# Prefix scan of a gated linear-attention trunk: rows reversed, modulation moved into the weights

## What is computed

```python
h = rmsnorm(x, norm1_g) * (1 + sc1) + sh1
k = h @ W_k ;  a = h @ W_a                        # 4 heads of 128; rank 16
la = log_sigmoid(a @ w_alpha + b_alpha) / 16      # one decay per key channel
S_t = exp(la_t)[:, None] * S_{t-1} + k_t^T v_t    # per head, 128 x 256
```

## Time and profile before

| | us |
|---|---|
| median of 3 executions | 1438.56 (1438.42 to 1439.32) |
| the profiled execution | 1442.98 |
| its span on the slowest core | 1441.4 |
| busy in it: PE, DVE, ACT, POOL | 1333.1, 688.4, 504.3, 109.8 |

### The profile page before, as it was taken

The page is one execution under the profiler, slowest core; times in us unless marked ns, Lnnn a source line. Parts: engine busy times, 40 slices in busy tenths (PEclk is TensorE's granted clock), DMA queues, the critical chain, the costliest instruction groups (busy, mean ns, idle before and its releaser), DMA issues.

```text
span 1441.4 us, 22660 instructions; the slowest of 8 cores (1428.5 to 1441.4 us)
## 1 busy us (share of the span) xinstructions
PE 1333.1 (92%) x7660; PEld 695.5 (48%) x7660; DVE 688.4 (48%) x1257; ACT 504.3 (35%) x1122; POOL 109.8 (8%) x208
## 2 busy tenths in 40 slices
PE   1577999998989899889999999999999999999997
PEld 1333445444545455544445555555555445555443
DVE  1467557543656577642233334962122552212486
ACT  1576456432445455431211112981111001111233
POOL 3000100000000000011110120010000002000000
PEclk9778999998999999999999999999999999999999
DMA  9736401206211111154342366532223006222222
GB/s 173 212 117 154 52 9 30 52 2 59 51 23 23 23 23 23 23 96 73 52 74 38 62 102 135 179 68 37 40 35 44 1 1 103 36 40 35 59 103 110
DMA packets 42797, 92.66 MB, mean 64 GB/s; under 512 B 5206, under 2 KB 8166, under 8 KB 42684
## 3 DMA queue, kind: packets, MB, share of 16 engines
q0 software_dynamic: 29264, 53.02, 24.9%
q1 hardware_dynamic: 13420, 38.20, 8.2%
HBM read 133.95 MB, written 10.25 MB: 100 GB/s over the span
## 4 chain that ended last, share of the span: by engine, by line
PE 74%; ACT 9%; DMA 5%; DVE 5%; issue 5%; POOL 0%; ACTq 0%; DVEq 0%; SPq 0%; POOLq 0%
PE psum L464 72%; ACT sb_arena L447 6%; DMA sb_wring<-wfm 2%; DVE sb_arena L450 2%; PE psum L467 2%; ACT sb_tmpB L447 2%; DMA sb_wring<-w_in 1%; ACT sb_rstd L447 1%; DMA sb_wring<-w_mod 1%; DVE sb_arena L454 1%; DVE sb_arena L458 1%; DMA sb_arena<-xm 1%; DVE sb_tmpB L458 0%; POOL sb_wring L437 0%; DVE sb_arena L455 0%
## 5 line engine op out<-in xcount | busy, mean ns | idle before, releaser
L464 PE MATMUL psum<-sb_arena,sb_wring 128*128 128x384 bf16 (+3 forms) x4448 | 837.5, 347 | 11.5 <-DVE sb_arena L461 10.1
L464 PEld LDWEIGHTS psum<-sb_arena,sb_wring 128*128 128x128 bf16 x4448 | 430.1, 98 | 385.3 <-issue 44.2
L464 PE MATMUL psum<-sb_wring,sb_arena 128*128 128x512 bf16 (+2 forms) x1596 | 350.4, 378 | 4.3 <-DMA sb_wring<-w_in 4.3
L447 ACT ACTIVATE sb_tmpB<-psum 128x384 f32<-128x384 f32 (+1 forms) x264 | 139.6, 532 | 606.3 <-PE psum L464 576.1
L450 DVE TENSOR_TENSOR sb_arena<-psum,sb_tmpB 128x384 bf16<-128x384 f32 (+5 forms) x254 | 148.6, 587 | 324.6 <-PE psum L464 306.1
L464 PEld LDWEIGHTS psum<-sb_wring,sb_arena 128*128 128x128 bf16 (+1 forms) x1596 | 155.8, 99 | 184.0 <-issue 7.4
L437 POOL DMA_DIRECT2D sb_wring<-wfm x140 | 75.3, 545 | 912.5 <-PE psum L464 769.0
L450 DVE TENSOR_TENSOR sb_tmpB<-psum,sb_tmpB 128x384 f32<-128x384 f32 (+2 forms) x80 | 47.8, 598 | 171.0 <-PE psum L464 170.5
L450 DVE TENSOR_TENSOR sb_arena<-psum,sb_arena 128x512 f32<-128x512 f32 (+2 forms) x106 | 72.6, 685 | 35.3 <-PE psum L464 35.1
L447 ACT ACTIVATE sb_arena<-sb_arena 128x1024 bf16<-128x1024 f32 (+2 forms) x60 | 60.5, 1010 | 76.7 <-DVE sb_arena L450 61.8
L467 PE MATMUL psum<-sb_identb,sb_arena 128*128 128x128 bf16 (+2 forms) x636 | 58.4, 234 | 24.6 <-DVE sb_arena L454 22.1
(11 more groups left out here) (94 smaller groups left out, 582.3 us busy)
## 6 DMA issues: line engine op xcount, KB each, us to landing
sb_wring<-wfm POOLq DMA_DIRECT2D x140, 256.0 KB, 6.1
sb_arena<-xm SPq DMA_DIRECT2D x29, 512.0 KB, 5.5
sb_arena<-xp SPq DMA_DIRECT2D x16, 512.0 KB, 8.2
ym<-sb_arena SPq DMA_DIRECT2D x16, 512.0 KB, 2.7
sb_wring<-w_ffn_out POOLq DMA_DIRECT2D x22, 256.0 KB, 4.6
sb_wring<-w_in POOLq DMA_DIRECT2D x16, 256.0 KB, 9.7
sb_wring<-w_mod POOLq DMA_DIRECT2D x16, 256.0 KB, 7.8
sb_wring<-w_o POOLq DMA_DIRECT2D x8, 256.0 KB, 8.0
```

Source lines behind the costliest of these rows:

```text
L447: return P.op("act", lambda e: e.activation(out=out, in_=in_, func=func, **kw), reads=reads, writes=writes)
L464: return P.op("pe", lambda e: e.matmul(out, lhsT=lhsT, rhs=rhs, start=start, stop=stop), reads=reads, writes=writes)
```

## The change

The host hands over the prefix rows in reverse order, so that a running sum from the first column (`car` carries it from block to block, `bcP` has a column more) is the decay of all later rows. Prefix blocks are transposed without the modulation, two feature tiles to one copy, into four buffers. The scale goes into `wam` and, in place, into the four key weights (`fold_h`, on POOL), the shift into the biases `ba` and `bk`, which are added as `aTp` and `kdP` are written. The Ln runs on two heads at once and the keys' Exp on four. The scaling of the rows from block 3 on moves from DVE to POOL, the copy to `kdtmP` from DVE to ACT, and the main rows' evictions from ACT to DVE except for the first bank of block 4. Blocks 0 and 1 are normed and transposed among the modulation weights. Each step is now two spreads: gates, keys and the scaling of rows first; transposes, `kdtmP` and squares second. The state starts at step 4, and the key weights are loaded again for the main rows.

```diff
--- before.py
+++ after.py
@@ -299,11 +299,11 @@
 
 
         xnP, r_xnP = ring("xnP", B0, 2048, 16, "pre")
-        for o_, n_ in ((C0, 3), (C0 + 30720, 2), (D0 + 16384, 2), (D0 + 37888, 4)):
+        for o_, n_ in ((C0, 3), (C0 + 30720, 2), (D0 + 16448, 2), (D0 + 37888, 4)):
             xa, xb = ring("xnQ%d" % o_, o_, 2048, n_, "pre")
             xnP, r_xnP = xnP + xa, r_xnP + xb
         hTp, r_hTp = [], []
-        for c_ in (1536, 512, 1024):
+        for c_ in (0, 512, 1024, 1536):
             hTp.append(hT[:, :, c_:c_ + 512])
             r_hTp.append([mreg("hTp%d_%d" % (c_, k), [(A0 + (k * TX + c_) * 2, A0 + (k * TX + c_ + 512) * 2)], "pre") for k in range(KT)])
         S32 = view(D0 + 34816, 4096, F32).rearrange("p (h v) -> p h v", h=NH)
@@ -317,9 +317,18 @@
             r_kdP.append([mreg("kdP%d_%d" % (i, h), [(o_ + h * 1024, o_ + (h + 1) * 1024)], "pre") for h in range(NH)])
         bcP, r_bcP = [], []
         for i in range(2):
-            o_ = D0 + i * 8192
-            bcP.append(view(o_, 8192, F32).rearrange("p (h t) -> p h t", h=NH))
-            r_bcP.append([mreg("bcP%d_%d" % (i, h), [(o_ + h * 2048, o_ + (h + 1) * 2048)], "pre") for h in range(NH)])
+            o_ = D0 + i * 8208
+            bcP.append(view(o_, 8208, F32).rearrange("p (h t) -> p h t", h=NH))
+            r_bcP.append([mreg("bcP%d_%d" % (i, h), [(o_ + h * 2052, o_ + (h + 1) * 2052)], "pre") for h in range(NH)])
+        o_ = C0 + 34816
+        wam = view(o_, 256).rearrange("p (k c) -> p k c", k=KT)
+        r_wam = mreg("wam", [(o_, o_ + 256)], "pre")
+        shb = view(o_ + 256, 16)
+        r_shb = mreg("shb", [(o_ + 256, o_ + 272)], "pre")
+        bk = view(o_ + 288, 16, F32)
+        r_bk = mreg("bk", [(o_ + 288, o_ + 304)], "pre")
+        ba = view(o_ + 320, 4, F32)
+        r_ba = mreg("ba", [(o_ + 320, o_ + 324)], "pre")
         kdtmP, r_kdtmP = ring("kdtmP", C0 + 6144, 1024, 16, "pre")
         GT = view(C0 + 6144, 8192).rearrange("p (k d) -> p k d", k=KT)
         r_GT = mreg("GT", [(C0 + 6144, C0 + 6144 + 8192)], "fin")
...
@@ -620,7 +629,7 @@
             act(rstd[:, c0:c1], rstd[:, c0:c1], AF.Exp, [r_rstd[gi]], [r_rstd[gi]], scale=-0.5)
             yield
             for j, (xi, xo, R) in enumerate(srcs):
-                ts(xnP[xo][0:R, :], xin[xi][0:R, :], rstd[0:R, c0 + j:c0 + j + 1], None, ALU.mult, None, [r_xin[xi], r_rstd[gi]], [r_xnP[xo]])
+                ts(xnP[xo][0:R, :], xin[xi][0:R, :], rstd[0:R, c0 + j:c0 + j + 1], None, ALU.mult, None, [r_xin[xi], r_rstd[gi]], [r_xnP[xo]], eng='dve' if i < 3 else 'pool')
                 if j % 2 == 1:
                     yield
 
@@ -637,6 +646,15 @@
                         tr(psb(b)[:, kk * 512 + c:kk * 512 + c + R], xnP[xo][0:R, k * 128:(k + 1) * 128], identb[0:R, 0:R],
                            [r_xnP[xo], r_identb], [r_ps[b]])
                         c += R
+                if i < NPB:
+                    o_, i_ = dst[:, kp * 2:kp * 2 + 2, 0:512], psb(b).rearrange("p (k c) -> p k c", k=2)
+                    dr = [dregs[kp * 2], dregs[kp * 2 + 1]]
+                    if i < 2 and kp % 2:
+                        act(o_, i_, AF.Copy, [r_ps[b]], dr)
+                    else:
+                        cp(o_, i_, [r_ps[b]], dr)
+                    yield
+                    continue
                 for kk in range(2):
                     k = kp * 2 + kk
                     runs = [(0, np_, 0)]
@@ -646,7 +664,7 @@
                         o_ = dst[:, k, col0 + c:col0 + c + n]
                         i_ = psb(b)[:, kk * 512 + c:kk * 512 + c + n]
                         rr = [r_ps[b], r_modT[1], r_modT[0]]
-                        if kp == 0 or (kp == 2 and i % 2):
+                        if kp == 0 and i < NPB + 1:
                             act(o_, i_, AF.Identity, rr, [dregs[k]], scale=modT[:, 1, k, seq:seq + 1], bias=modT[:, 0, k, seq:seq + 1])
                         else:
                             ts(o_, i_, modT[:, 1, k, seq:seq + 1], modT[:, 0, k, seq:seq + 1], ALU.mult, ALU.add, rr, [dregs[k]])
@@ -654,53 +672,81 @@
 
         def norm_t(i):
             if i < NPB:
-                return norm_b(i, hTp[i % 3], r_hTp[i % 3], 0)
+                return norm_b(i, hTp[i % 4], r_hTp[i % 4], 0)
             g = i - NPB
             return norm_b(i, hT, [r_hT[k][g] for k in range(KT)], GRP[g][0])
 
 
         def blk_tiles(i):
             if i < NPB:
-                return [(xp[((NPB - 1 - i) * 4 + j) * 128:((NPB - 1 - i) * 4 + j + 1) * 128, :], 128) for j in range(4)]
+                return [(xp[(i * 4 + j) * 128:(i * 4 + j + 1) * 128, :], 128) for j in range(4)]
             return [(xm[t * 128:(t + 1) * 128, :], 128) if t < NPT else (xs[:, :], 64) for t in GTILES[i - NPB]]
 
         xts = {}
+
+        def fold_a():
+
+            cp(shb, modT[:, 0, :, 0], [r_modT[0]], [r_shb])
+            tt(wam, wa[:], modT[:, 1, :, 0:1].broadcast_to([128, KT, 16]), ALU.mult, [r_wa, r_modT[1]], [r_wam])
+            b = newbank()
+            for k in range(KT):
+                mm(psf(b)[0:16, 0:1], wa[:, k, :], shb[:, k:k + 1], k == 0, k == KT - 1, [r_wa, r_shb], [r_ps[b]])
+            cp(ba[0:16, :], psf(b)[0:16, 0:1], [r_ps[b]], [r_ba])
+
+        def fold_h(h, wk):
+            b = newbank()
+            for k in range(KT):
+                mm(psf(b)[:, 0:1], wk[h].lhs(k), shb[:, k:k + 1], k == 0, k == KT - 1, [wk[h].reg, r_shb], [r_ps[b]])
+            cp(bk[:, h:h + 1], psf(b)[:, 0:1], [r_ps[b]], [r_bk])
+            wr = wring[:, wk[h].s, :].rearrange("p (k d) -> p k d", k=KT)
+            tt(wr, wr, modT[:, 1, :, 0:1].broadcast_to([128, KT, 128]), ALU.mult, [wk[h].reg, r_modT[1]], [wk[h].reg], eng="pool")
+
+        def halo():
+
+            for c in range(2):
+                tt(ulastP[:, :, c:c + 1], hTp[0][:, :, 1 - c:2 - c], modT[:, 1, :, 0:1], ALU.mult, r_hTp[0] + [r_modT[1]], [r_ulastP])
+            tt(hT[:, :, TM:TX], ulastP[:], modT[:, 0, :, 0:1].broadcast_to([128, KT, 2]), ALU.add, [r_ulastP, r_modT[0]], [r_hTh])
 
         def pre_gate(pb):
 
             st = pb % 2
             b = newbank()
             for k in range(KT):
-                mm(psf(b)[0:16, :], wa[:, k, :], hTp[pb % 3][:, k, :], k == 0, k == KT - 1, [r_wa, r_hTp[pb % 3][k]], [r_ps[b]])
-            cp(aTp[:, st, :], psf(b)[0:16, :], [r_ps[b]], [r_aTp[st]])
+                mm(psf(b)[0:16, :], wam[:, k, :], hTp[pb % 4][:, k, :], k == 0, k == KT - 1, [r_wam, r_hTp[pb % 4][k]], [r_ps[b]])
+            ts(aTp[:, st, :], psf(b)[0:16, :], ba[0:16, 0:1], None, ALU.add, None, [r_ps[b], r_ba], [r_aTp[st]])
+            if pb == 0:
+                P.op("dve", lambda e: e.memset(car[:], 0.0), writes=[r_car])
+            cp(bcP[st][:, :, 0:1], car[:].unsqueeze(2), [r_car], r_bcP[st])
             yield
-            for h in range(NH):
-                ti = rot("tmpB", NT4)
+
+            def scan(h):
+                P.op("dve", lambda e: e.tensor_tensor_scan(out=bcP[st][:, h, 1:513], data0=consts[:, 1:2].broadcast_to([128, 512]), data1=tmpB[:, h, :],
+                                                           initial=car[:, h:h + 1], op0=ALU.mult, op1=ALU.add),
+                     reads=[r_consts, r_tmpB[h], r_car], writes=[r_bcP[st][h]])
+
+            for h in range(NH):
                 b = newbank()
                 mm(psf(b), walpha[:, h * 128:(h + 1) * 128], aTp[:, st, :], True, True, [r_walpha, r_aTp[st]], [r_ps[b]])
-                act(tmpB[:, ti, :], psf(b), AF.Exp, [r_ps[b], r_nbal], [r_tmpB[ti]], scale=-1.0, bias=nbal[:, h:h + 1])
-                act(tmpB[:, ti, :], tmpB[:, ti, :], AF.Ln, [r_tmpB[ti], r_consts], [r_tmpB[ti]], bias=consts[:, 1:2])
-                P.op("dve", lambda e, h=h, ti=ti: e.tensor_tensor_scan(out=bcP[st][:, h, :], data0=consts[:, 1:2].broadcast_to([128, 512]), data1=tmpB[:, ti, :],
-                                                                        initial=0.0, op0=ALU.mult, op1=ALU.add),
-                     reads=[r_consts, r_tmpB[ti]], writes=[r_bcP[st][h]])
+                act(tmpB[:, h, :], psf(b), AF.Exp, [r_ps[b], r_nbal], [r_tmpB[h]], scale=-1.0, bias=nbal[:, h:h + 1])
+                if h % 2:
+                    act(tmpB[:, h - 1:h + 1, :], tmpB[:, h - 1:h + 1, :], AF.Ln, [r_tmpB[h - 1], r_tmpB[h], r_consts], [r_tmpB[h - 1], r_tmpB[h]], bias=consts[:, 1:2])
+                if h >= 2:
+                    scan(h - 2)
                 yield
-
-            if pb == 0:
-                ts(nbP[:, st, :], bcP[st][:, :, 511], -1.0 / 16, None, ALU.mult, None, r_bcP[st], [r_nbP[st]])
-            else:
-                stt(nbP[:, st, :], bcP[st][:, :, 511], -1.0 / 16, nbP[:, 1 - st, :], ALU.mult, ALU.add, r_bcP[st] + [r_nbP[1 - st]], [r_nbP[st]])
+            scan(2)
+            scan(3)
+            cp(car[:].unsqueeze(2), bcP[st][:, :, 512:513], r_bcP[st], [r_car])
             yield
 
         def pre_keys(pb, wk):
 
             st = pb % 2
```

(92 more changed lines are left out.)

2 lines of the change are left out of this document (1 added, 1 removed).

## The result

The changed kernel is slower: 1449.86 us, median of five runs, against 1439.32 for the kernel before beside it, a ratio of 1.0065 with a 95% interval of 1.0043 to 1.0087. The forecast was 1413.7 in a range from 1403 to 1427: the sign was wrong, and the miss is 36 us.

A forecast was written before the change was run, and what follows sets the result against it. It took DMA to bound the kernel to 42.3 us, no engine to 143.65, then PE. Stretches of 45 + 32.5 + 16 + 16 + 11 + 48.5 = 169 for 193.9 us give −24.9, from 1438.56 to 1413.7, range 1403 to 1427.

The forecast's parts named there:

- The scaling on POOL: Blocks 3 to 8, 21 tiles: 1.6 us each (0.74 to 2.45), covered by the first half of a step.
- POOL becomes the bound: Rival, 0.06: 21 scaling tiles form one chain from 75.5 us; at 5 us a tile +9.6 us, 1448.2.
- Steps 3 to 6: Step 3, without gates, PE-bound: 11 us for 11.8; steps 4 to 6 up to `qk_h`: 48.5 for 50.25.
- The start: From the modulation to the end of step 0: 32.5 us for 50.9, 18.4 less.
- the 4.54 us wait has its cause removed: Argument against the chain rival: the rank-16 product's wait for a modulated copy behind DVE's scans goes away.
- rank-16 product already issued, keys in line: First half of steps 1 and 2: with this order DVE ends its last scan at 14.4 us of a 16 us step.
- The head: Modulation with blocks 0 and 1: DMA-bound, +2.7 us, ends at 45; PE's product order there costs nothing.
- Steps 1 and 2: Steps with gates, ACT fullest at 14.7 us: 16 us each for 20.6 and 18.05, −4.6 and −2.0.
- Without gaps: Rival, 0.13: ACT runs without gaps and steps take the fullest engine's work; −34.8 us, 1403.8.
- It does not do what it says: Rival, 0.05: late weight load in `qk_h` or block 1's transposes delaying modulation gives back half the gain; 1426.
- The chain stays: Rival, 0.14: each gate's chain through PE, ACT and DVE sets the steps; only the start gains, 15.7 us, 1422.9.
- POOL and DVE exclude each other: Rival, 0.12: scans wait for POOL tiles in progress, costing 13 to 16 us, partly in slack; −12 us, 1426.

The follow-up runs named there:

- the kernel with the early `Exp`: Kernel without elementwise work on POOL, keys' fused Exp issued among the squares of the step before: `qk_h` starts at 179.4 us, against 180.0.
- the head edits: On the kernel without POOL work: modulation products before block 1's squares and transposes; first gate's first piece before `fold_h`; both. `qk_h` starts at 179.8, 182.1, 182.9 us.
- the experiment on the order: Changed kernel, POOL work kept, next block's squares in one go ahead of the transposes: `qk_h` starts at 191.3 and 191.6 us, against 201.4.
- the best kernel: Early-`Exp` kernel without POOL work, first head's key products ahead of the next gate's rank-16 product in steps 1 and 2: 1422.09 us, 0.987 of before.

## Why the prediction was wrong

By the prediction's own terms, on the profiled core (us; forecast, then measured): to the last modulation product 45, 48.1; from there to the end of step 0 32.5, 44.1; step 1 16, 16.4; step 2 16, 15.2; step 3 11, 16.0; steps 4 to 6 48.5, 62.9. Sum 169, 202.7. Three terms carry the miss.

**The scaling on POOL.** The step that failed is "Even 2.45 (9.8 us) is mostly covered; that is +1 a step in the range". Two things were wrong in it. The price: 2.83 us a tile, above the upper bound of 2.45, which was the rate of DVE's scan; nothing in the rows said that POOL could not be slower per element than DVE's slowest instruction. And, worth more, the cover: I set four tiles against the *length* of the half step beside them, instead of following who waits for the last tile and who makes the next block's first. The rival named "POOL becomes the bound" had the right mechanism and the right side, but it priced POOL's tiles as one open chain, 75.5 + 21p + 23. At the measured 2.83 that gives 157.9, and by it POOL would have been harmless up to 4.5 us. Measured is 44.8 us more, and the POOL timeline says where they are: block 3's statistics came at 88.56, 13.1 later than 75.5; four gaps between blocks, 7.89 + 6.31 + 5.41 + 8.85 = 28.5; 0.9 in the tiles; 2.3 in the tail. The gaps are the loop. A chain whose own input hangs on its output must be priced by the turn (tiles + transposes + evictions + squares), not by its tiles. Steps 3 to 6, forecast 59.5, took 78.9; the same steps without POOL work (123.47 to 183.57 in that kernel) 60.1. So those two terms were right but for POOL, and their whole miss is POOL's.

**The start.** 44.1 for 32.5, and without POOL work still 41.6 (50.1 to 91.7), so what runs on POOL is not the main cause. The first gate came as forecast: 13 us from the modulation to its last scan in the sum (45 to 58), 13.6 without POOL work (48.9 to 62.4, medians of the cores). Left out were two hand-overs behind it, at which PE waits with keys queued behind the wait. The first is the second gate's product with `walpha`. It needs `aTp`, and DVE's copy of that stands behind the first gate's scans and the four products on the key weights, or the delay that these cause from POOL (*exclude each other*, below). In the changed kernel:

```profile
71.39 0.58 PE L473 MATMUL psum<-sb_aTp,sb_walpha 16*128 16x512 bf16 x1 [11.75 <-DVE sb_arena L470]
```

That PE waits 11.75 us there was not in the sum (8.9 us and more without POOL work); nor that PE then runs its next products at the lower clock level:

```profile
71.40:76.00 4.60, 4.60 (x11) 1.23 (x12) 0.31 (x1) 2.49 (x2) 0.00 (x0) 0.50 0.00 0
```

A granted clock of 0.50 is 1.2 GHz. The sum also had the products on the key weights run on POOL from 53 us; they began at 58.2 to 60.4, and on four of the eight cores the wait is put down to block 2's rows, which hold the first key weight as told above.

The second hand-over is the third gate's: 3.30 us ahead of its rank-16 product, then 1.0 for `aTp`. The profile puts the 3.30 down to ACT's last square, and that is not the releaser. In the kernel with the early `Exp` that square ends 2.6 us ahead of the product instead of 0.1, yet the wait is as long and has another name (core 2):

```profile
88.25 3.53 PE L473 MATMUL psum<-sb_arena 128*16 128x512 bf16 x8 [3.30 <-DVE sb_arena L470]
```

In both kernels, on all cores but one, the product starts 0.26 us after DVE's first paired copy of block 2, which stands behind the gate's last two scans. That is the place where the modulated copy of the earlier trace rows stood. So the argument "the 4.54 us wait has its cause removed" failed: the copies lost their modulation and kept their place, and the wait became 3.30 us here and 1.59 in the next step. The phrase that failed with it is "rank-16 product already issued, keys in line": it is issued first, but it waits, and the keys in line wait with it. Keys ahead of it were worth 6.7 us at the qk start (172.7 against 179.4).

**The head.** 48.1 for 45. The DMA term was right: with the products ahead of the transposes, the cores read 45.0 to 46.7. The note that failed is the one that costed PE's order at nothing: it looked at md 8 behind block 0's transposes, not at the last product behind block 1's. It cost the forecast 2 to 3 us but the kernel none, as the head edits gained nothing at the qk start.

**What was right.** Steps 1 and 2 took 16.4 and 15.2 us for 16 each, with ACT 13.2 (forecast 14.7), DVE 12.1 (11.2) and a granted clock of 1.00 in step 1. The pair holds without POOL work too (18.15 and 13.65); that each came near 16 is partly luck, as both hold the waits of the second hand-over, which the working did not have. The prices that had a near row held (the fused `Exp`'s row is above):

```profile
L470 DVE COPY sb_arena<-psum 128x1024 bf16<-128x1024 bf16 x12 | 7.7, 687 | 3.4 <-PE psum L476 3.4
L456 ACT ACTIVATE sb_tmpB<-sb_tmpB,sb_consts 128x1024 f32<-128x1024 f32 x8 | 9.2, 1148 | 0.7
```

The paired copy took 0.687 us for 0.683, so the Trainium skill's rule of 1x for matmul output ("VectorE: DVE Perf Modes", Rules for kernel authors), an estimated 1.1, does not hold for it. `Ln` of 1024 took 1.15 for 1.15, the fused `Exp` 1.90 for 1.95. The reloaded key weights, issued at 177.3 behind POOL's tiles, made no wait in `qk_h`, and the part behind changed by 0.6 us on the slowest core. The error was not in instruction prices but in one engine without a row and in what is queued behind a wait.

**The other rivals.** *Without gaps*: no. *It does not do what it says*: block 1's transposes did hold back the modulation, at no cost in the end. *The chain stays*: half of it came true, as the hand-over between gate and keys set the start even without POOL. *POOL and DVE exclude each other*: real. In the changed kernel `fold_h`'s products on POOL meet the first gate's scans on DVE, cores 2 and 4, timeline of each:

```profile
56.08 4.85 DVE L723 TENSOR_TENSOR_SCAN sb_arena<-sb_consts,sb_car,sb_tmpB 128x512 f32<-128x512 f32 x4 [2.98 <-ACT sb_tmpB L456]
60.36 7.86 POOL L459 TENSOR_TENSOR sb_wring<-sb_wring,sb_modT 128x1024 bf16<-128x1024 bf16 x4 [20.10 <-DVE sb_arena L723]
63.41 2.97 DVE L459 TENSOR_TENSOR sb_ulastP<-sb_arena,sb_modT 128x8 f32<-128x8 bf16 x2
66.49 1.77 DVE L459 TENSOR_TENSOR sb_arena<-sb_ulastP,sb_modT 128x16 bf16<-128x16 f32 x1
```

```profile
57.65 9.62 DVE L723 TENSOR_TENSOR_SCAN sb_arena<-sb_consts,sb_car,sb_tmpB 128x512 f32<-128x512 f32 x4 [2.98 <-ACT sb_tmpB L456]
58.64 10.33 POOL L459 TENSOR_TENSOR sb_wring<-sb_wring,sb_modT 128x1024 bf16<-128x1024 bf16 x4 [18.64 <-DMA sb_arena<-xp]
67.37 1.62 DVE L470 COPY sb_car<-sb_arena 128x4 f32<-128x4 f32 x1
```

On core 2 POOL starts when the scans are nearly through, and four scans take 4.85 us; on core 4 it starts after the first, and they take 9.62, each of three 1.6 longer. The eight cores show 4.85, 6.45 or 9.62 (one reads 6.48), that is in steps of 1.6 us, and nothing between. By that the trace agrees with the lock that the Trainium skill describes in "SBUF — State Buffer", section SBUF: two separate sides. (The kernel with only `fold_h` on POOL has cores at 8.02 too.) On core 2 the price is not gone but falls on `halo`'s small products behind the scans: 2.97 and 1.77 us, where they take 0.43 and 0.18 on core 4. From the first scan to the second `aTp` DVE's queue takes 12.1 to 12.8 us on all eight cores, and 10.8 on all eight when DVE makes the products itself. With 4.9 us for the products that leaves an estimated 5.9 for the rest, so from POOL they cost DVE 6.2 us or more, and 4.9 if it makes them itself. At the qk start the offload loses 3.2 us (the kernels with and without `fold_h` on POOL, the scaling on DVE), where the rival had 12.

Beside the one-input scaling tiles it is otherwise. In step 2 all four scans start while POOL works (107.75 to 120.06): one takes 1.87 us for 1.25, the other three 1.27 to 1.3, so the forecast wait of a whole tile for each scan is refuted there, and the lock does not show. Why the one is longer stays open.

Open too: of the 18.2 us that the scaling on POOL costs, the experiment on the order accounts for 10; that the other 8 are the longer latency of a block by itself is argued, not shown. And of the forecast's 169, the best kernel reached 172.7. Its trace still has PE waiting 8.9 to 10.2 us at the first hand-over, which no edit removed; whether the 4 us left are there was not tried.

## What to carry to other kernels

Before an operation goes to an engine that computes nothing yet, draw the turn it stands in: who waits for its last tile, and what must that one do before the operation's next input is ready; if the answer leads back to the operation, its full length counts, however idle the engine is beside it. Price an engine without a row by an open upper bound, and let the forecast's sign depend on it. And in a software pipeline look at what is *queued behind* each waiting instruction: work whose inputs are all there belongs ahead of the product that waits, and that order was worth 6.7 us here, where the fused exponentials were worth none. And when a profile names the releaser of a wait, check it on a kernel in which that one ends earlier: here the wait stayed.

## What the runs showed of the hardware

- The scaling of a 128x1024 tile, f32 in, bf16 out, by one value a partition: 2.83 us on POOL, 0.743 on DVE. By "GPSIMD Engine Reference", Elementwise — side-by-side cycle accounting, of the Trainium skill it would be an estimated 1.5; the measurement decides.
- The product of 128x1024 bf16 with a broadcast operand: 1.21 us on DVE; on POOL 1.97 (7.86 / 4) to 2.6 (10.33 / 4), the more scans it meets. DVE works beside it in every run, so its price alone is not shown.
- POOL's product and DVE's scan hold each other up, 1.6 us for each scan met; even a copy of four elements took 1.62 us there and 0.17 elsewhere. The one-input tile on POOL leaves three of four scans alone, but DVE's own scaling tile beside it takes 1.5 to 1.6 us for 0.74.
- One `Exp` over 2048 columns took 1.90 us, four over 512 2.46 (4 x 0.616).
